# Splitting 18 more branch slabs of a two-block layer, and making 38 low parts with an accumulating transfer

## The chip, the cores and the metric

The program runs on one core of one Trainium2 chip. The metric is the device time of one execution in microseconds, the median of several runs. The numbers of the profile come from one profiled execution.

## The reference

The reference is two blocks of a language model over 256 tokens of width 2048, all in float32. The first block is a normalised input projection (2048 to 8192), a short gated convolution, attention with eight heads, and an output projection. The second block, where the change lies, computes:

```
h        = rmsnorm(x)
proj     = h @ w_in_2                     # 2048 -> 2048 (conv) + 1024 (ssm) + 4096 (gates)
b_conv   = silu(layernorm(conv31(glu(proj[:2048])))) @ conv_w_out
b_ssm    = (z @ w_val) * sigmoid(z @ w_gate),  z = gelu(state-space scan of proj[2048:3072])
gates    = sigmoid(proj[3072:] + b_gate)
x        = x + (gates0 * b_conv + gates1 * b_ssm) @ w_out
x        = x + peer(rmsnorm(x))           # picks 128 rows of a table for each token, twice
out      = rmsnorm(x)
```

## The kernel before

**Slabs.** Every weight matrix is cut into slabs of 128 partitions x 2048 float32 (1 MB). SP loads them one after the other (`load`, L356) into four buffers of `weight_raw`; the load of slab n waits until TensorE has finished the slab n-4. `weight_low` is declared over the same bytes as `weight_raw`. One slab gives one tile of 128 output channels x 256 tokens, summed over 16 blocks of the contraction.

**Two ways to multiply.** A plain tile (`tile`, L468) is 16 float32 matmuls of raw weight and operand. A split tile makes the same product out of float32r parts: the weight is high + low, the operand is high + low, and the tile is high*high + high*low + low*high. `split_product` issues 32 matmuls with the high part (L488, L489), and then, behind a wait on the low part, 16 matmuls with it (L492). `wide_product` (L508, L511) does the same with a double-width operand in other stages.

**Who makes the parts.** ACT makes the high part with a rounding copy from `weight_raw` into one of two buffers of `weight_high` (`split_high`, L761), once TensorE has finished the split tile two before. DVE subtracts it from the raw slab in place and so gives the low part (`split_low`, L1108).

**The branch and gate stages.** The first 24 slabs of `w_in_2` are the branch tiles, in the order of the list `BRANCH`: four conv tiles, ssm 0 to 3, twelve conv tiles, ssm 4 to 7. Twenty are plain; four (t = 6 to 9, from `SPLIT_AT`) are split. The 32 gate slabs behind them are all split. ACT goes through the tiles in order: `read_out` (L796) copies the finished tile out of PSUM, then `split_high` makes the high part of a slab that comes two later. After the branch tiles 5 to 8, TensorE multiplies the ssm inputs (L632) and ACT copies them out of PSUM (`ssm_inputs`, L761 on `work`). In the gate stage TensorE has extra work after gate 1 (`ssm_outputs`), gates 5 to 8 (`ssm_inputs`), gate 19 and gate 23 (layer-norm sums, L675 and L681).

**DVE beside them.** DVE's order is written out by hand: operand lows (L1389), convolution of two channels with their `split_low` calls, the first scan (L1406 to L1411, from `scan(0)`), three more convolutions (L1441) with the lows of gates 0 to 18 between the taps, then `scan(1)` with the lows of gates 19 to 31. Each `split_low` waits for ACT's high part of its slab. TensorE waits for DVE at gate 19 (`conv_done`), at `ssm_outputs(0)` after gate 1 and at `ssm_outputs(1)` after the 14th tile of the following stage.

**GpSimd.** POOL makes constants at the start and is then idle until the table rows are gathered (`gather`, L428: an indirect transfer of 128 rows of 8 KB, 1 MB, each).

Of the kernel before, what the change touches and what calls it, by code (L numbers as in the profile page):

```python
# [13 lines left out]
P = 128  # L14
# [48 lines left out]
def uses_before(b, s):  # L63
# [25 lines left out]
PLAIN = 2  # L89
SPLIT_OUT = 64 - PLAIN  # L90
SPLIT_BRANCH = SPLIT_OUT + 16
SPLIT_GATE = SPLIT_BRANCH + 4
SPLIT_VG = SPLIT_GATE + 32
SPLIT_OUT2 = SPLIT_VG + 16
SPLIT_AT = 6
SPLIT_SLABS = [*range(PLAIN, 80), *range(80 + SPLIT_AT, 80 + SPLIT_AT + 4), *range(80 + 24, 80 + 56), *range(80 + 56 + 8, 80 + 56 + 8 + 32)]
SPLIT_TILES = [*range(TILE_IN + PLAIN, TILE_IN2), *range(TILE_IN2 + SPLIT_AT, TILE_IN2 + SPLIT_AT + 4), *range(TILE_GATE, TILE_CV),
               *range(TILE_VG + 1, TILE_OUT2, 2), *range(TILE_OUT2, TILE_WQ)]

O_OUT, O_GATE, O_Z, O_OUT2 = KD, 2 * KD, 3 * KD, 3 * KD + KH  # L100


def split_in(t):

    return t - PLAIN


def split_tile(i):
# [4 lines left out]
def split_slab(i):  # L113

    return SPLIT_SLABS[i]

# [66 lines left out]
def build(nc, d):  # L183
    ctx = ExitStack()
    with ctx:
# [3 lines left out]
        def sem(name):  # L189
            return ctx.enter_context(nc.semaphore(name))  # L190
# [99 lines left out]
        eps_ready = sem("eps_ready")  # L290
        x_paired, x_squared = sem("x_paired"), sem("x_squared")
        proj_done, proj_freed = sem("proj_done"), sem("proj_freed")
        w_high_ready, w_low_ready = sem("w_high_ready"), sem("w_low_ready")
        o_high_ready, o_low_ready = sem("o_high_ready"), sem("o_low_ready")
        misc_done, misc_freed = sem("misc_done"), sem("misc_freed")
        bu_done, bu_freed, cy_done, skip_ready = sem("bu_done"), sem("bu_freed"), sem("cy_done"), sem("skip_ready")
# [108 lines left out]
        @block.gpsimd  # L405
        def _(pool):
            nc.gpsimd.memset(ident[:, :], 0.0).then_inc(consts_set, 1)
            nc.gpsimd.memset(ones[:, :], 1.0).then_inc(consts_ready, 1)
            pool.wait_ge(consts_set, 1)
            nc.gpsimd.affine_select(out=ident[:, :], in_=ident[:, :], compare_op=ALU.not_equal, fill=1.0, base=0,  # L410
                                    pattern=[[-1, P]], channel_multiplier=1).then_inc(consts_ready, 1)
            nc.gpsimd.memset(mask, 0.0).then_inc(mask_set, 1)
            pool.wait_ge(mask_set, 1)
            for lo in (0, 2 * P):
                nc.gpsimd.affine_select(out=mask[:, lo:lo + P], in_=mask[:, lo:lo + P], compare_op=ALU.is_ge,
                                        fill=-3.0e38, base=0, pattern=[[-1, P]],
                                        channel_multiplier=1).then_inc(mask_ready, 1)

            pool.wait_ge(merged, KD)
            nc.gpsimd.iota(iota16, pattern=[[1, 16]], base=0, channel_multiplier=0,  # L420
                           allow_small_or_imprecise_dtypes=True).then_inc(zero_ready, 1)
            nc.gpsimd.memset(zero_row, 0.0).then_inc(zero_ready, 1)
            def gather(s, col, table):

                b = ROW[s]
                if USES[s] > 0:
                    pool.wait_ge(row_free[b], USES[s])
                nc.gpsimd.indirect_dma_start(  # L428
                    rows[b], None, table, bass.IndirectOffsetOnAxis(ap=picks[:, col:col + 1], axis=0),
                ).then_inc(gathered[b], 16)  # L430

            for t in range(TT):
                for v, table in ((0, d["peer_u_2"][0]), (1, d["peer_v_2"][0])):
                    parts = [(*heads, n + 1) for n, heads in enumerate(HEAD_PARTS)] if t == v == 0 \
                        else [(0, PEER_H, len(HEAD_PARTS) + t)]
                    for first, last, ready in parts:
                        pool.wait_ge(picks_ready, ready)
                        for i in range(first * PEER_K, last * PEER_K):
                            s = (2 * t + v) * PICKS + i
                            if UNPACED <= s < EARLY_PICKS:  # L440
                                slab = SLAB_WQ + slab_before(s)
                                pool.wait_ge(raw_landed[slab % NSLAB], 16 * (slab // NSLAB + 1))
                            if s == EARLY_PICKS:
                                pool.wait_ge(proj_done, TILES)
                            gather(s, t * PICKS + i, table)
# [5 lines left out]
        def _(pe):  # L451
# [20 lines left out]
            def split_product(i, sub=0, kts=KD, order=None, ready=None, place=lambda k: k):  # L472

                per = SLAB // kts // P
                t = split_tile(i) - (per - 1) + sub
                if sub == 0:
                    slabs.append(t)
                at = split_slab(i) % NSLAB
                high, low = (w.rearrange("p (k n) -> p k n", k=kts)[:, :, sub * P:(sub + 1) * P]
                             for w in (w_high[:, i % NHIGH, :], w_low[:, at, :]))  # L480
                out = ps_p[:, (t - TILE_IN) % PSLOTS, :]
                order = list(range(kts)) if order is None else order
                pe.wait_ge(w_high_ready, i + 1)
                pe.wait_ge(proj_freed, t + 1)
                for k in order:
                    if ready is not None:
                        pe.wait_ge(o_low_ready, ready(k))
                    nc.tensor.matmul(out, high[:, k, :], o_high[:, place(k), :], start=(k == order[0]), stop=False)  # L488
                    nc.tensor.matmul(out, high[:, k, :], o_low[:, place(k), :], start=False, stop=False)  # L489
                pe.wait_ge(w_low_ready, i + 1)  # L490
                for k in order:
                    mm = nc.tensor.matmul(out, low[:, k, :], o_high[:, place(k), :], start=False, stop=(k == order[-1]))  # L492
                mm.then_inc(proj_done, 1)

            def wide_product(i, order=None, ready=None, place=lambda k: k):
# [9 lines left out]
                for k in order:  # L505
                    if ready is not None:
                        pe.wait_ge(o_low_ready, ready(k))
                    nc.tensor.matmul(out, high[:, k, :], o_parts[:, :, place(k), :], start=(k == order[0]), stop=False)  # L508
                pe.wait_ge(w_low_ready, i + 1)
                for k in order:  # L510
                    mm = nc.tensor.matmul(out[:, 1, :], low[:, k, :], o_high[:, place(k), :], start=False, stop=(k == order[-1]))  # L511
                mm.then_inc(proj_done, 1)
# [138 lines left out]
            pe.wait_ge(misc_freed, M_B + 4)  # L651
            first = BRANCH.index(("ssm", 0)) + 1
            for t in range(len(BRANCH)):
                if SPLIT_AT <= t < SPLIT_AT + 4:
                    split_product(SPLIT_BRANCH + t - SPLIT_AT, ready=(lambda k: O_GATE + k + 1) if t == SPLIT_AT else None)
                else:
                    tile(TILE_IN2, t, normed_in, ready=(lambda k: (h_scaled, KD + k + 1)) if t == 0 else None)
                if first <= t < first + 4:
                    ssm_inputs(t - first)

# [98 lines left out]
        def _(act):  # L759
# [8 lines left out]
            def split_high(i):  # L768

                s = split_slab(i)  # L770
                act.wait_ge(raw_landed[s % NSLAB], 16 * (s // NSLAB + 1))
                if i >= NHIGH:
                    act.wait_ge(proj_done, split_tile(i - NHIGH) + 1)
                act_copy(w_high[:, i % NHIGH, :], w_raw[:, s % NSLAB, :]).then_inc(w_high_ready, 1)

            def square(n, q0, src):

# [170 lines left out]

            first = BRANCH.index(("ssm", 0)) + 1
            for t, (kind, n) in enumerate(BRANCH):  # L950
                read_out(TILE_IN2, t, slot(BRANCH_SLOT[kind] + n), ACT.Sigmoid if kind == "sig" else ACT.Copy)
                if t in (SPLIT_AT - 3, SPLIT_AT - 2):
                    split_high(SPLIT_BRANCH + t - SPLIT_AT + 3)
                elif t in (SPLIT_AT, SPLIT_AT + 1):
                    split_high(SPLIT_BRANCH + t - SPLIT_AT + 2)
                if first <= t < first + 4:
                    ssm_inputs(t - first)
                elif first + 4 <= t < first + 8:
                    if t == first + 4:
                        act.wait_ge(rstd_ready, 12)  # L960
                    skip_matrix(t - first - 4)
                if t >= len(BRANCH) - 2:
                    split_high(SPLIT_GATE + t - (len(BRANCH) - 2))

            for t in range(32):
                dst = slot(GA0 + t) if t < KD else slot(gb(t - KD))
                read_out(TILE_GATE, t, dst, ACT.Sigmoid, bias=params[:, C_GATE + t:C_GATE + t + 1])
                if t < 30:
                    split_high(SPLIT_GATE + t + 2)
                if SSM_IN <= t < SSM_IN + 4:  # L970
                    ssm_inputs(t - SSM_IN + 4)
                elif t == SSM_OUT + 1:
# [99 lines left out]
        def _(dve):  # L1072
# [30 lines left out]

            def split_low(i):

                s = split_slab(i)
                dve.wait_ge(w_high_ready, i + 1)
                v.tensor_tensor(w_low[:, s % NSLAB, :], w_raw[:, s % NSLAB, :], w_high[:, i % NHIGH, :], ALU.subtract).then_inc(w_low_ready, 1)  # L1108
# [383 lines left out]
            for k in range(KD):  # L1492
                operand_low(O_GATE + k + 1, normed_in[:, k, :], k)
            conv(0, 1, 0, ())
            split_low(SPLIT_BRANCH)
            conv(1, 1, 0, ())
            for n in range(1, 4):
                split_low(SPLIT_BRANCH + n)
            scan(0)
            conv(2, 2, 0, LOW_LAGS[0])  # L1500
            conv(4, 2, 5, LOW_LAGS[1])
# [239 lines left out]
```

## Time and profile before

| what | value |
|---|---|
| median of 3 runs | 2513.13 us (2512.08 to 2514.20) |
| profiled execution | 2512.88 us, span 2511.1 us |
| PE busy | 1733.7 us (69%) |
| DVE busy | 1872.3 us (75%) |
| ACT busy | 564.1 us (22%) |
| POOL busy | 869.5 us (35%) |
| DMA | 747.83 MB, 51.5% of the engines' time for POOL's transfers, 22.9% for SP's |

The page averages over very different stages: projections up to about 1050 us, the routing and the gathers after that. The change touches the stretch from 515 to 888 us of the span (branch tiles, then gate tiles), so the rows are read there.

### The profile page before, as it was taken

What the parts mean: (1) busy time and instruction counts of PE and PEld (TensorE: products, weight loads), DVE (VectorE), ACT (ScalarE), POOL (GpSimd) and SP (SyncE); (2) the same over time, 40 slices, a digit from 0 to 9 for tenths busy, and PEclk for the clock granted to TensorE, in tenths of its full rate; (3) what the DMA queues carried; (4) which work ended last, traced back from release to release, by engine and by line L of the source; (5) the groups of instructions that cost most, each with busy time, mean ns of one, the idle gap of its engine ahead of it and who ended that gap; (6) DMA issues with size and microseconds to landing.
All of it is one profiled execution on the core that took longest, in us unless ns stands there. A gap on an engine that the chain in (4) does not pass through costs nothing. (4 is left out here: it accounts for less than half of the span.)

```text
span 2511.1 us, 22450 instructions
## 1 busy us (share of the span) xinstructions
PE 1733.7 (69%) x8754; PEld 1310.6 (52%) x8754; DVE 1872.3 (75%) x2486; ACT 564.1 (22%) x832; POOL 869.5 (35%) x524
## 2 busy tenths in 40 slices
PE   9999999999999999999920004777750000277776
PEld 8888887889889989888810001222220000022222
DVE  7757687688989885565999997777469999844444
ACT  4345555432143524432000001000000000100000
POOL 0000000000000000001458886655558888755552
PEclk9999999999999999999965557999985555599999
DMA  6544444534445444555989999999999999999997
GB/s 231 185 168 168 168 168 151 201 136 153 161 141 183 160 159 154 192 192 211 411 327 422 422 422 422 422 421 421 422 421 423 422 422 422 422 422 421 422 422 302
DMA packets 103495, 747.83 MB, mean 298 GB/s; under 512 B 11616, under 2 KB 11616, under 8 KB 12896
## 3 DMA queue, kind: packets, MB, share of 16 engines
q0 software_dynamic: 73728, 536.90, 51.5%
q1 hardware_dynamic: 29376, 209.20, 22.9%
q8 instruction: 69, 1.13, 0.2%
q10 hardware_dynamic: 288, 0.31, 0.0%
q14 instruction: 34, 0.28, 0.0%
HBM read 744.28 MB, written 2.10 MB: 297 GB/s over the span
## 5 line engine op out<-in xcount | busy, mean ns | idle before, releaser
L1108 DVE TENSOR_TENSOR weight_low<-weight_raw,weight_high 128x2048 fp32r<-128x2048 f32 x146 | 334.0, 2288 | 119.7 <-ACT weight_high L761 119.6
L747 PE MATMUL ps<-weight_raw,residual_t 128*128 128x512 f32 x368 | 171.3, 609 | 323.0 <-ACT residual_t L1058 265.0
L508 PE MATMUL ps<-operand_parts,weight_high 128*128 128x512 f32 x1504 | 370.9, 399 | 8.0 <-DVE operand_parts L1360 3.9
L420 POOL IOTA slots<- 128x16 f32 x1 | 0.1, 144 | 1043.3 <-DVE slots L1486 1043.3
L747 PE MATMUL ps<-rows_high,residual_t 128*128 128x512 f32 x192 | 92.2, 625 | 347.9 <-ACT residual_t L1058 317.4
L508 PEld LDWEIGHTS ps<-operand_parts,weight_high 128*128 128x128 f32 x1504 | 279.4, 189 | 70.5 <-issue 5.5
L761 ACT ACTIVATE weight_high<-weight_raw 128x2048 fp32r<-128x2048 f32 x146 | 278.6, 1908 | 97.1 <-PE ps L511 94.5
L747 PEld LDWEIGHTS ps<-weight_raw,residual_t 128*128 128x128 f32 x368 | 67.2, 192 | 427.2 <-ACT residual_t L1058 332.9
L747 PEld LDWEIGHTS ps<-rows_high,residual_t 128*128 128x128 f32 x192 | 36.1, 198 | 403.8 <-ACT residual_t L1058 347.7
L468 PE MATMUL ps<-slots,weight_raw 128*128 128x256 f32 x960 | 208.3, 379 | 0.9 <-DVE slots L1119 0.9
L488 PE MATMUL ps<-operand_parts,weight_high 128*128 128x256 f32 x832 | 204.2, 285 | 0.0
L489 PE MATMUL ps<-operand_parts,weight_high 128*128 128x256 f32 x832 | 202.5, 283 | 0.0
L1593 DVE SCALAR_TENSOR_TENSOR weight_raw<-weight_raw,work 128x2048 f32<-128x2048 f32 x85 | 193.4, 2290 | 11.7 <-DMA weight_raw<-in_peer_u,slots 11.7
L511 PEld LDWEIGHTS ps<-operand_parts,weight_low 128*128 128x128 f32 x1504 | 192.8, 191 | 7.5 <-DVE weight_low L1108 0.3
L468 PEld LDWEIGHTS ps<-slots,weight_raw 128*128 128x128 f32 x960 | 182.0, 190 | 26.2 <-issue 1.6
L511 PE MATMUL ps<-operand_parts,weight_low 128*128 128x256 f32 x1504 | 195.2, 283 | 0.0
L428 POOL DMA_INDIRECT weight_raw<-in_peer_u,slots x85 | 172.8, 2033 | 29.4 <-issue 25.3
L1593 DVE SCALAR_TENSOR_TENSOR slots<-slots,work 128x2048 f32<-128x2048 f32 x75 | 170.6, 2290 | 9.5 <-DMA slots<-in_peer_u,slots 9.4
L1611 DVE SCALAR_TENSOR_TENSOR work<-weight_raw,slots,work 128x2048 f32<-128x2048 f32 x45 | 105.8, 2352 | 93.9 <-DMA weight_raw<-in_peer_v,slots 93.6
L428 POOL DMA_INDIRECT slots<-in_peer_u,slots x75 | 147.9, 1973 | 59.5 <-issue 20.4
L428 POOL DMA_INDIRECT weight_raw<-in_peer_v,slots x91 | 129.7, 1425 | 99.5 <-PE ps L747 74.0
L488 PEld LDWEIGHTS ps<-operand_parts,weight_high 128*128 128x128 f32 x832 | 159.5, 192 | 3.2 <-issue 3.1
(230 smaller groups left out, 2950.4 us busy)
## 6 DMA issues: line engine op xcount, KB each, us to landing
weight_raw<-in_w_in SPq DMA_DIRECT2D x120, 1024.0 KB, 4.8
weight_raw<-in_w_out SPq DMA_DIRECT2D x32, 1024.0 KB, 4.8
weight_raw<-in_peer_w_q SPq DMA_DIRECT2D x16, 1024.0 KB, 8.5
weight_raw<-in_conv_w_out SPq DMA_DIRECT2D x8, 1024.0 KB, 4.8
weight_raw<-in_ssm_w_val SPq DMA_DIRECT2D x8, 1024.0 KB, 4.8
weight_raw<-in_ssm_w_gate SPq DMA_DIRECT2D x8, 1024.0 KB, 4.8
residual_t<-in_x SPq DMA_DIRECT2D x4, 512.0 KB, 5.9
out_y<-work SPq DMA_DIRECT2D x4, 512.0 KB, 5.2
```

The costliest lines, as they stand in the source:

```text
L420: nc.gpsimd.iota(iota16, pattern=[[1, 16]], base=0, channel_multiplier=0, allow_small_or_imprecise_dtypes=True).then_inc(zero_ready, 1)
L428: nc.gpsimd.indirect_dma_start(rows[b], None, table, bass.IndirectOffsetOnAxis(ap=picks[:, col:col + 1], axis=0),).then_inc(gathered[b], 16)
L468: mm = nc.tensor.matmul(ps_p[:, t % PSLOTS, :], w[:, k, :], operand[:, k, :], start=(k == order[0]), stop=(k == order[-1]))
L488: nc.tensor.matmul(out, high[:, k, :], o_high[:, place(k), :], start=(k == order[0]), stop=False)
L489: nc.tensor.matmul(out, high[:, k, :], o_low[:, place(k), :], start=False, stop=False)
L508: nc.tensor.matmul(out, high[:, k, :], o_parts[:, :, place(k), :], start=(k == order[0]), stop=False)
L511: mm = nc.tensor.matmul(out[:, 1, :], low[:, k, :], o_high[:, place(k), :], start=False, stop=(k == order[-1]))
L747: mm = nc.tensor.matmul(ps_v[:, c, :], diag[:, i // 2 % 16, :], rows[b][:, c * 512:(c + 1) * 512], start=False, stop=False, skip_group_che ...
L761: return nc.scalar.activation(dst, src, ACT.Copy)
L1108: v.tensor_tensor(w_low[:, s % NSLAB, :], w_raw[:, s % NSLAB, :], w_high[:, i % NHIGH, :], ALU.subtract).then_inc(w_low_ready, 1)
L1593: v.scalar_tensor_tensor(out=rows[b], in0=rows[b], scalar=1.0, in1=h_tok[:, t, :], op0=ALU.mult, op1=ALU.mult, accum_out=dots[:, at:at + 1 ...
L1611: v.scalar_tensor_tensor(out=y_tok[:, t, :], in0=rows[b], scalar=pick_w[:, at:at + 1], in1=y_tok[:, t, :], op0=ALU.mult, op1=ALU.add).then ...
```

## The change

The branch tiles 2 to 23 are split now (before: 6 to 9), so 22 instead of 4. For these 22 and for the gates 0, 2, ... 30 DVE's subtraction is left out. ACT writes the negated high part into the `weight_high` buffer; POOL then issues a transfer that loads the same slab from memory once more and adds it to what is in that buffer, which leaves the low part there. ACT makes the high part a second time, in place in the raw slab's buffer, after it has read the finished tile out. TensorE swaps the two buffers for these slabs and waits for the transfer's semaphore in place of DVE's.

```diff
-SPLIT_GATE = SPLIT_BRANCH + 4
+SPLIT_GATE = SPLIT_BRANCH + 22
+PLAIN2 = 2
+SPLIT_SLABS = [*range(PLAIN, 80), *range(80 + PLAIN2, 80 + 56), *range(80 + 56 + 8, 80 + 56 + 8 + 32)]
+LOW_BY_DMA = [*range(SPLIT_BRANCH, SPLIT_GATE), *range(SPLIT_GATE, SPLIT_VG, 2)]
...
+def lows_by_vector(i):
+    return i + 1 - sum(j <= i for j in LOW_BY_DMA)
...
+            for n, i in enumerate(LOW_BY_DMA):
+                t = split_tile(i) - TILE_IN2
+                kind, m = BRANCH[t] if t < len(BRANCH) else ("gate", t - len(BRANCH))
+                pool.wait_ge(minus_high, n + 1)
+                nc.gpsimd.dma_start(w_high[:, i % NHIGH, :], d["w_in_2"][BRANCH_SLAB.get(kind, 3 * KH) + m],
+                                    accum_op=ALU.add).then_inc(low_landed[i % NHIGH], 16)
...
+                parts = (w_low[:, at, :], w_high[:, i % NHIGH, :]) if by_dma else (w_high[:, i % NHIGH, :], w_low[:, at, :])
-                pe.wait_ge(w_low_ready, i + 1)
+                if by_dma:
+                    pe.wait_ge(low_landed[i % NHIGH], 16 * sum(j <= i and (i - j) % NHIGH == 0 for j in LOW_BY_DMA))
+                else:
+                    pe.wait_ge(w_low_ready, lows_by_vector(i))
...
+            def split_minus_high(i):
+                s = split_slab(i)
+                act.wait_ge(raw_landed[s % NSLAB], 16 * (s // NSLAB + 1))
+                act.wait_ge(proj_done, split_tile(i - NHIGH) + 1)
+                nc.scalar.activation(w_high[:, i % NHIGH, :], w_raw[:, s % NSLAB, :], ACT.Copy, scale=-1.0).then_inc(minus_high, 1)
+            def split_in_place(i):
+                s = split_slab(i)
+                act_copy(w_low[:, s % NSLAB, :], w_raw[:, s % NSLAB, :]).then_inc(w_high_ready, 1)
+            def read_and_split(i, tile0, n, dst, func=ACT.Copy, **kw):
+                if i in LOW_BY_DMA:
+                    split_minus_high(i)
+                    read_out(tile0, n, dst, func, **kw)
+                    split_in_place(i)
+                else:
+                    read_out(tile0, n, dst, func, **kw)
+                    if i < SPLIT_VG:
+                        split_high(i)
...
             def split_low(i):
+                if i in LOW_BY_DMA:
+                    return
...
             conv(0, 1, 0, ())
-            split_low(SPLIT_BRANCH)
             conv(1, 1, 0, ())
-            for n in range(1, 4):
-                split_low(SPLIT_BRANCH + n)
             scan(0)
```

The loops over the branch and gate tiles on ACT call `read_and_split` with the slab two tiles ahead.

## Rows read from the trace of the kernel before

**Rows 1.** The page: clock and DMA in 40 slices, queues
```profile
PEclk9999999999999999999965557999985555599999
DMA  6544444534445444555989999999999999999997
...
q0 software_dynamic: 73728, 536.90, 51.5%
q1 hardware_dynamic: 29376, 209.20, 22.9%
```
**Rows 2.** Windows: us, PE, PEld, DVE, ACT, POOL busy (count), clock, DMA share, GB/s
```profile
515.00:681.00 166.00, 166.00 (x897) 147.39 (x896) 147.43 (x307) 34.31 (x65) 0.00 (x0) 1.00 0.41 146
681.00:888.00 207.00, 205.44 (x1710) 197.03 (x1709) 182.92 (x306) 94.73 (x108) 0.00 (x0) 1.00 0.46 163
```
**Rows 3.** Timeline of ACT, branch stage: start, duration, what, idle before
```profile
572.62 2.05 ACT L761 ACTIVATE work<-ps 128x512 f32<-128x512 f32 x4
...
591.50 0.38 ACT L796 ACTIVATE slots<-ps 128x256 f32<-128x256 f32 x1 [6.24 <-PE ps L468]
...
598.40 0.38 ACT L796 ACTIVATE slots<-ps 128x256 f32<-128x256 f32 x1 [6.23 <-PE ps L468]
...
563.52 0.38 ACT L796 ACTIVATE slots<-ps 128x256 f32<-128x256 f32 x1 [3.85 <-PE ps L492]
...
570.54 0.38 ACT L796 ACTIVATE slots<-ps 128x256 f32<-128x256 f32 x1 [2.88 <-PE ps L492]
```
**Rows 4.** Timeline of ACT, gate stage
```profile
775.13 0.47 ACT L796 ACTIVATE slots<-ps,scan_ws 128x256 f32<-128x256 f32 x1 [3.48 <-PE ps L492]
775.50 1.91 ACT L761 ACTIVATE weight_high<-weight_raw 128x2048 fp32r<-128x2048 f32 x1
780.89 0.47 ACT L796 ACTIVATE slots<-ps,scan_ws 128x256 f32<-128x256 f32 x1 [3.48 <-PE ps L492]
```
**Rows 5.** Waits between 680 and 900 us: total, times, longest
```profile
DVE weight_low L1108 <- ACT weight_high L761: 22.9, 11, 7.2
...
PEld ps L492 <- DVE weight_low L1108: 1.8, 1, 1.8
```
**Rows 6.** Timelines of DVE (ends of convolutions and second scan) and of ACT
```profile
797.00 0.14 DVE L1503 COPY small<-small 128x1 f32<-128x1 f32 x1
...
813.14 0.38 ACT L977 ACTIVATE scan_ws<-ps 128x256 f32<-128x256 f32 x1 [1.18 <-PE ps L675]
...
932.09 0.15 DVE L1426 COPY small<-small 128x1 f32<-128x1 f32 x1
...
935.87 0.38 ACT L796 ACTIVATE operand<-ps 128x256 f32<-128x256 f32 x1 [3.07 <-PE ps L468]
```
**Rows 7.** Groups of DVE, 515 to 952 us
```profile
L1108 DVE TENSOR_TENSOR weight_low<-weight_raw,weight_high 128x2048 fp32r<-128x2048 f32 x38 | 86.8, 2286 | 27.6 <-ACT weight_high L761 27.5
```
**Rows 8.** Timeline of PE: one gate tile, its high part and its low part
```profile
700.67 0.39 PE L488 MATMUL ps<-operand_parts,weight_high 128*128 128x256 f32 x1
...
704.61 2.08 PE L492 MATMUL ps<-operand_parts,weight_low 128*128 128x256 f32 x16
706.52 0.28 PE L488 MATMUL ps<-operand_parts,weight_high 128*128 128x256 f32 x1
```
**Rows 9.** Source line 428, POOL's gathers of 1 MB: time from issue to landing
```profile
DMA to landing us min/median/max: 5.7/23.8/26.8
```
**Rows 10.** Timeline of POOL, first gathers
```profile
1172.82 0.94 POOL L428 DMA_INDIRECT rows_high<-in_peer_u,slots  x1 [0.30 <-issue]
```
**Rows 11.** DMA between 1300 and 1400 us: queue, packets, MB, share of 16 engines
```profile
q0 software_dynamic: 5750, 41.87, 101.1%
```
**Rows 12.** DMA between 515 and 681 us: queue, then SP's issues with us to landing
```profile
q1 hardware_dynamic: 3312, 24.12, 40.6%
...
weight_raw<-in_w_in SPq DMA_DIRECT2D x23, 1024.0 KB, 4.8
```
**Rows 13.** Timeline of ACT around gate 27
```profile
864.85 1.91 ACT L761 ACTIVATE weight_high<-weight_raw 128x2048 fp32r<-128x2048 f32 x1
866.78 1.28 ACT L987 ACT_TABLE_LOAD   x1
868.07 3.31 ACT L987 ACTIVATE slots<-slots,scan_ws 128x256 f32<-128x256 f32 x8
871.40 1.28 ACT L796 ACT_TABLE_LOAD   x1
```

More of the change, by code:

```diff
@@ L91 @@
 SPLIT_BRANCH = SPLIT_OUT + 16
-SPLIT_GATE = SPLIT_BRANCH + 4
+SPLIT_GATE = SPLIT_BRANCH + 22
 SPLIT_VG = SPLIT_GATE + 32
 SPLIT_OUT2 = SPLIT_VG + 16
-SPLIT_AT = 6
-SPLIT_SLABS = [*range(PLAIN, 80), *range(80 + SPLIT_AT, 80 + SPLIT_AT + 4), *range(80 + 24, 80 + 56), *range(80 + 56 + 8, 80 + 56 + 8 + 32)]
-SPLIT_TILES = [*range(TILE_IN + PLAIN, TILE_IN2), *range(TILE_IN2 + SPLIT_AT, TILE_IN2 + SPLIT_AT + 4), *range(TILE_GATE, TILE_CV),
+PLAIN2 = 2
+SPLIT_SLABS = [*range(PLAIN, 80), *range(80 + PLAIN2, 80 + 56), *range(80 + 56 + 8, 80 + 56 + 8 + 32)]
+SPLIT_TILES = [*range(TILE_IN + PLAIN, TILE_IN2), *range(TILE_IN2 + PLAIN2, TILE_CV),
                *range(TILE_VG + 1, TILE_OUT2, 2), *range(TILE_OUT2, TILE_WQ)]
+LOW_BY_DMA = [*range(SPLIT_BRANCH, SPLIT_GATE), *range(SPLIT_GATE, SPLIT_VG, 2)]
 O_OUT, O_GATE, O_Z, O_OUT2 = KD, 2 * KD, 3 * KD, 3 * KD + KH
@@ L292, in build @@
         proj_done, proj_freed = sem("proj_done"), sem("proj_freed")
-        w_high_ready, w_low_ready = sem("w_high_ready"), sem("w_low_ready")
+        w_high_ready, w_low_ready, minus_high = sem("w_high_ready"), sem("w_low_ready"), sem("minus_high")
+        low_landed = [sem(f"low_landed{n}") for n in range(NHIGH)]
         o_high_ready, o_low_ready = sem("o_high_ready"), sem("o_low_ready")
@@ L478, in split_product @@
                 at = split_slab(i) % NSLAB
-                high, low = (w.rearrange("p (k n) -> p k n", k=kts)[:, :, sub * P:(sub + 1) * P]
-                             for w in (w_high[:, i % NHIGH, :], w_low[:, at, :]))
+                by_dma = i in LOW_BY_DMA
+                parts = (w_low[:, at, :], w_high[:, i % NHIGH, :]) if by_dma else (w_high[:, i % NHIGH, :], w_low[:, at, :])
+                high, low = (w.rearrange("p (k n) -> p k n", k=kts)[:, :, sub * P:(sub + 1) * P] for w in parts)
                 out = ps_p[:, (t - TILE_IN) % PSLOTS, :]
@@ L508, in wide_product @@
                     nc.tensor.matmul(out, high[:, k, :], o_parts[:, :, place(k), :], start=(k == order[0]), stop=False)
[L509 removed]
+                pe.wait_ge(w_low_ready, lows_by_vector(i))
                 for k in order:
@@ L653, in _ @@
             for t in range(len(BRANCH)):
-                if SPLIT_AT <= t < SPLIT_AT + 4:
-                    split_product(SPLIT_BRANCH + t - SPLIT_AT, ready=(lambda k: O_GATE + k + 1) if t == SPLIT_AT else None)
+                if t < PLAIN2:
+                    tile(TILE_IN2, t, normed_in, ready=(lambda k: (h_scaled, KD + k + 1)) if t == 0 else None)
                 else:
-                    tile(TILE_IN2, t, normed_in, ready=(lambda k: (h_scaled, KD + k + 1)) if t == 0 else None)
+                    split_product(SPLIT_BRANCH + t - PLAIN2, ready=(lambda k: O_GATE + k + 1) if t == PLAIN2 else None)
                 if first <= t < first + 4:
@@ L950, in _ @@
             for t, (kind, n) in enumerate(BRANCH):
[L951 to L955, printed above, removed]
+                read_and_split(SPLIT_BRANCH + t, TILE_IN2, t, slot(BRANCH_SLOT[kind] + n), ACT.Sigmoid if kind == "sig" else ACT.Copy)
                 if first <= t < first + 4:
@@ L961, in _ @@
                     skip_matrix(t - first - 4)
-                if t >= len(BRANCH) - 2:
-                    split_high(SPLIT_GATE + t - (len(BRANCH) - 2))
             for t in range(32):
                 dst = slot(GA0 + t) if t < KD else slot(gb(t - KD))
-                read_out(TILE_GATE, t, dst, ACT.Sigmoid, bias=params[:, C_GATE + t:C_GATE + t + 1])
-                if t < 30:
-                    split_high(SPLIT_GATE + t + 2)
+                read_and_split(SPLIT_GATE + t + 2, TILE_GATE, t, dst, ACT.Sigmoid, bias=params[:, C_GATE + t:C_GATE + t + 1])
                 if SSM_IN <= t < SSM_IN + 4:
```

## The prediction

> **What bounds the kernel now.** I read the page first. From about 1250 us on the DMA line stands at eight or nine tenths [rows 1]: that half is gathers, the change does not touch it, and it starts only when the projections are done. So what the projections lose or gain should reach the end one for one. Then the windows of the two stages touched [rows 2]. In the branch stage (515 to 681 us) PE is busy 166.00 of 166 us, in the gate stage 205.44 of 207, both at a granted clock of 1.00, which is the 2.4 GHz level. DVE has 147.43 and 182.92 us of work, ACT far less, POOL none, and the DMA engines are busy 0.41 and 0.46 of the time. So TensorE's stream of matmuls is the bound, and everything else is cover. The waits confirm it: in the gate stage PE waited once for a low part, 1.8 us, while DVE waited 22.9 us for ACT's high parts [rows 5]. DVE follows PE there, it does not hold it back. Its two late deadlines hold too: the convolutions end at 797.0 us, and PE's sum over them, which asks for them, ends just before ACT reads it at 813.1; the second scan ends at 932.1 us, and the tile ahead of its use is read out at 935.9 [rows 6].
>
> **What the split itself gives.** A plain branch tile takes 598.40 - 591.50 = 6.90 us from one read-out to the next. A gate tile, which is split, takes 780.89 - 775.13 = 5.76 us [rows 3, 4]. A split branch tile with ssm inputs takes 570.54 - 563.52 = 7.02, so 1.26 us are the inputs [rows 3]. Eighteen more split tiles save 18 x (6.90 - 5.76) = 20.5 us, if PE waits for nothing new. The stage is then 2 x 6.90 + 22 x 5.76 + 4 x 1.26 = 145.6 us, against 20 x 6.90 + 4 x 5.76 + 4 x 1.26 = 166.1 before, which agrees with the window.
>
> **DVE** drops 20 subtractions: 36 before in these stages (4 branch, 32 gates; the 38 of the group include two of a later stage), 16 after. At 2.29 us each that is 46 us less work [rows 7]. This pays nothing on its own, as PE did not wait for DVE, but for the 1.8 us. It is what lets DVE's two deadlines come 20 us earlier: the odd gates' lows still wait for PE, the rest does not.
>
> **ACT.** Each of the 38 slabs takes a second copy of 1.9 us, 72 us in all. ACT's cycle per tile becomes 1.9 + 0.4 + 1.9 = 4.2 us in 5.76 [rows 4], or 6.3 of 7.02 beside the ssm inputs with their 2.05 us of copies [rows 3]. The high part is ready 4.2 us after the tile two before has ended, and PE asks at 5.76. So it is hidden, with 1.5 us to spare. The read-out is 1.9 us later and PE needs its PSUM bank only a whole tile later. The cover is gone in one place: at gate 27 ACT spends 5.9 us on table loads and eight Silu [rows 13]; I put 1 us there.
>
> **SP** issues as before. Its buffers are freed by the same tiles. **POOL** is idle, so the 38 issues queue behind nothing.
>
> **The new wait.** This carries the whole forecast. PE now waits, between the high part and the low part of a tile, for a chain: tile i-2 ends, ACT negates (1.9), POOL issues, the transfer lands (L), PE does 16 low matmuls. The high part of a tile takes 704.61 - 700.67 = 3.94 us and the low part 1.91 [rows 8]. So the low part is asked for 5.76 + 3.84 = 9.6 us after tile i-2 has ended, and L may be 9.6 - 1.9 - 0.1 = 7.6 us. Everything behind the waiting low matmuls on PE's queue waits too. The trace of before shows no accumulating transfer. The nearest row is a gather of the same 1 MB: 5.7 us from issue to landing at best, 0.94 of it POOL's own time [rows 9, 10]. With L = 5.7 the transfer is in time by 1.9 us. But an adding transfer also reads what it adds to: 1 MB from memory, 1 MB from SBUF, 1 MB written. In the saturated stretch 41.87 MB took 101.1% of 100 us, 2.53 us of all 16 engines per slab [rows 11]; a second read at that price makes L = 8.2, late by 0.6 us. The raw load of each slab overlaps in part and takes its turns on the same engines: half of its 2.9 us (40.6% of 166 us for 23 slabs [rows 12]) would be 1.4 more. The chain holds two tiles together: (1.9 + 0.1 + L + 1.9)/2 is 6.05 us per tile at L = 8.2 and 6.75 at 9.6.
>
> The second limit is the engines' own load. In the branch stage each tile brings a raw load and an adding one: 2.9 + 2 x 2.53 = 8.0 us of all engines if reads and writes add up wholly, 2.9 + 2.53 = 5.4 if the second read costs nothing. Both ends stay for the range. I take 7.0 us per tile, between the chain's 6.75 and the load's 8.0 and nearer to the chain, since part of the 2.9 us in a half-idle stage is waiting that a full queue would fill. In the gates two raw loads and one adding load take 2.9 x 2 + 5.1 = 10.9 of 11.5 us, so there the chain decides. I take L = 8.7 there: a pair of tiles takes 12.6 instead of 11.5 us, 1.1 lost. Of 16 pairs six have extra matmuls of 1.26 us or more in their window (the chain behind gates 0, 4, 6, 8, 18 and 22), which hide it. Ten remain.
>
> The Trainium skill, page "Collectives: The Full Stack", Part 3, section on the bandwidth ceiling, speaks against this change: the add inside the DMA engine costs nothing by itself, but its two source reads halve the rate. No run so far of this kernel shows it. By that rule the second read is paid in full (L = 8.2 and more); by the gather row alone it is not, and the sum is that of rival A.
>
> **Sum.** Branch: 2 x 6.90 + 22 x 7.0 + 4 x 1.26 = 172.8 against 166.1, +6.7 us. Gates: 10 x 1.1 = +11.0, less the 1.8 us that PE no longer waits, plus 1 at gate 27. Together +16.9 us on the profiled execution's 2512.9 us (span 2511.1), which lies 0.2 us under the median. That gives 2530 us.
>
> **Rivals.** A: the transfer is in time. The second read is hidden under the first, L stays at or under 7.6, and the stage runs at 5.76 us. For it: 5.7 us in rows 9, and DMA engines that are idle more than half of the time. Against it: the doubled reading. Then -20.5 - 1.8 = -22.3, 2490.6 us. This decides the sign: with nothing lost in the gates, the turn is at 6.78 us per branch tile ((166.1 - 18.8 + 1.8)/22).
>
> B: the adding transfer is far slower than two copies (row by row, read then write, little overlapped). From L = 12 on, a tile takes 8.0 us in the branch stage: +28.6 us, and each of the 16 gate pairs loses 4.4 us, 70 us less some 15 hidden: about 2595 us. Nothing in the trace excludes it; nothing shows it.
>
> C: PE's new gaps cost clock. In the second half of the page the clock falls to 5 where PE has nothing to do, from 9 where it works [rows 1]. Gaps of 1 to 2 us in each 7 are much shorter than those; but if the 1.2 GHz level came for a tenth of the two stages, each of those 37 us would do half its work, +19 us on top: 2549. The gate stage kept 1.00 with 1.6 us idle [rows 2].
>
> D: the edit has no effect on the sum: the branch stage turns from PE-bound to DMA-bound at about 6.8 us and the gates just keep up. Within 5 us of 2513.
>
> E: the transfer does not do what it says (each issue split in several, or POOL slow to build it, 3 us and more instead of 0.94). It would read as B in a weaker form, 2540 to 2570 us.
>
> **How the numbers follow.** 0.2% is 5 us, about what a measurement of this kernel can tell from no change. Chances: my case with its spread above +5 us 0.30; its lower edge where the branch stage gains a few us, faster than -5, 0.07; D 0.13; A 0.31; B 0.09; C 0.03; E 0.07. Faster 0.38, same 0.13, slower 0.49. The likeliest single case is mine, 2530. Its own range is 2505 (6.4 us per branch tile, gates level) to 2560 (8.0 us per tile: 194.8 us, +28.7, and gates +18). The whole range takes in A, 2488, and goes up through C and E to 2575; B's far end is left out.
>
> **What would show it.** In the profile after, PE's wait before the low matmuls L492 should be put down to a DMA into `weight_high`, 0.5 to 1.5 us per branch tile and about 1 us for every second gate. ACT's read-outs should be about 7.0 us apart in the branch stage, in the gates 11.5 to 12.6 for a pair. The branch window should show a DMA share above 0.85 against 0.41, and POOL's issues a landing of 8 to 10 us. DVE should have 20 subtractions fewer and finish its second scan earlier. If the landing is under 7.6 us, my second read is wrong and A has come. If the branch tiles lie 8 us and more apart with DMA engines not full, it is B. A clock under 0.95 in 515 to 900 us is C. A stall before L488, on the high part, would mean that I mispriced ACT.

## The result, and the profile after

The changed kernel takes 2550.77 us (median of 4 runs, 2543.03 to 2560.02) against 2513.66 before: ratio 1.0148, 95% interval 1.0135 to 1.0161. The profiled execution took 2551.71 us, its span is 2549.9 us. The change makes the kernel 37 us slower; its four runs scatter over 17 us, so the time is known to some 3 us (the interval). The forecast was 2530 us: the right sign, and less than half of the size.

The page after, clock and DMA in 40 slices, queues, and the group of the new transfers (answers to [rows 1]):

```profile
PEclk9999999999999999999985555999995555599999
DMA  5544444589978754554989999999999999999997
...
q0 software_dynamic: 79200, 576.75, 58.7%
q1 hardware_dynamic: 29376, 209.20, 22.3%
...
weight_high<-in_w_in POOLq DMA_DIRECT2D x38, 1024.0 KB, 10.3
```

The new part is the hump of 8, 9, 9, 7, 8, 7 in the DMA line, where 4 and 5 stood. POOL's queue moved 39.85 MB more, 38 slabs. The transfers of the two stages land a median of 10.3 us after POOL's issue.

The windows of the two stages after, in the columns of [rows 2]:

```profile
516.20:701.00 184.80, 155.97 (x1183) 148.11 (x1183) 139.38 (x309) 107.79 (x106) 19.93 (x23) 0.96 0.97 258
701.00:920.00 219.00, 204.16 (x1655) 193.76 (x1654) 143.51 (x257) 120.88 (x121) 12.78 (x15) 0.98 0.78 224
```

PE is no longer the bound of the branch stage: 156 us of work in 184.8 us, with the DMA engines busy 0.97 of the time. The granted clock is below 1.00 in both stages, which it was not before.

ACT's timeline after, the tiles around the end of the branch stage, the last gate, and POOL's first gather (answers to [rows 3, 4]; the last row is POOL's timeline):

```profile
694.14 1.92 ACT L799 ACTIVATE weight_high<-weight_raw 128x2048 fp32r<-128x2048 f32 x1 [3.74 <-PE ps L510]
695.97 0.36 ACT L837 ACTIVATE slots<-ps 128x256 f32<-128x256 f32 x1
696.23 1.90 ACT L779 ACTIVATE weight_low<-weight_raw 128x2048 fp32r<-128x2048 f32 x1
701.41 0.38 ACT L837 ACTIVATE slots<-ps 128x256 f32<-128x256 f32 x1 [3.28 <-PE ps L510]
...
926.58 0.47 ACT L837 ACTIVATE slots<-ps,scan_ws 128x256 f32<-128x256 f32 x1 [5.29 <-PE ps L510]
```
```profile
1210.20 1.05 POOL L442 DMA_INDIRECT rows_high<-in_peer_u,slots  x1 [124.75 <-DVE slots L1607]
```

The same three points in the trace of the kernel before:

```profile
681.28 0.39 ACT L796 ACTIVATE slots<-ps 128x256 f32<-128x256 f32 x1 [4.72 <-PE ps L468]
...
887.52 0.47 ACT L796 ACTIVATE slots<-ps,scan_ws 128x256 f32<-128x256 f32 x1 [5.29 <-PE ps L492]
```
```profile
1171.42 1.09 POOL L428 DMA_INDIRECT rows_high<-in_peer_u,slots  x1 [125.02 <-DVE slots L1575]
```

The first three ACT rows after the change are its cycle: negate, read out, copy in place. The last branch tile is read out at 701.41 us; before it was 681.28. Of the 20.1 us between, 1.2 had already come before the stage (the table load ahead of the first block's last square starts at 505.69 instead of 504.51; why is not shown), so the branch stage costs 18.9. The last gate is read out at 926.58 against 887.52, so the gates cost another 18.9. The first gather starts 38.8 us later than before (1210.20 against 1171.42), and the spans differ by 38.8. So next to nothing is won or lost behind the gates.

The waits after, first 516 to 701 us, then 701 to 922 us (answers to [rows 5]):

```profile
PEld ps L510 <- DMA weight_high<-in_w_in: 33.1, 21, 3.5
DVE scan_ws L1441 <- ACT work L779: 28.5, 1, 28.5
...
PE ps L510 <- DMA weight_high<-in_w_in: 28.4, 17, 3.3
```
```profile
PEld ps L510 <- DMA weight_high<-in_w_in: 17.0, 11, 2.9
PE ps L510 <- DMA weight_high<-in_w_in: 14.8, 10, 2.7
```

L510 is the line of the low matmuls, so this is the new wait where the prediction put it. PE waits 28.4 us in the branch stage for 22 slabs and 14.8 us in the gates. DVE gained the time that it was meant to gain and spends it waiting: 28.5 us ahead of its first scan alone (5.7 before), since PE delivers the ssm inputs too late. So its second scan ends at 969.1 us and not, as forecast, earlier than the 932.1 of before.

### The profile page after: what moved, and what is told of

The parts are those of the page before. It is cut to its first block and busy times, and to the rows that moved or that the text cites. A ratio compares the mean times of both kernels' runs of the same rounds, so it can differ in the third digit from the quotient of the medians.

```text
span 2549.9 us, 23117 instructions
## 1 busy us (share of the span) xinstructions
PE 1738.4 (68%) x9042; PEld 1319.2 (52%) x9042; DVE 1829.0 (72%) x2466; ACT 666.4 (26%) x888; POOL 910.7 (36%) x562
## 5 line engine op out<-in xcount | busy, mean ns | idle before, releaser
L1143 DVE TENSOR_TENSOR weight_low<-weight_raw,weight_high 128x2048 fp32r<-128x2048 f32 x126 | 288.5, 2290 | 176.3 <-ACT weight_high L779 176.3
L430 POOL DMA_DIRECT2D weight_high<-in_w_in x38 | 32.7, 861 | 876.1 <-ACT weight_high L799 876.1
L526 PEld LDWEIGHTS ps<-operand_parts,weight_high 128*128 128x128 f32 x1504 | 278.6, 189 | 69.9 <-issue 5.0
L779 ACT ACTIVATE weight_high<-weight_raw 128x2048 fp32r<-128x2048 f32 x126 | 240.4, 1908 | 94.5 <-PE ps L529 94.5
L529 PE MATMUL ps<-operand_parts,weight_low 128*128 128x256 f32 x1504 | 195.2, 283 | 0.0
L1091 ACT ACTIVATE residual_t<-ident,slots 128x128 f32<-128x128 f32 x128 | 48.1, 398 | 432.9 <-PE ps L765 432.1
L765 PE MATMUL ps<-slots,residual_t 128*128 128x512 f32 x272 | 126.3, 607 | 40.3 <-DMA slots<-in_peer_v,slots 40.3
L503 PE MATMUL ps<-operand_parts,weight_low 128*128 128x256 f32 x608 | 150.7, 288 | 0.0
L504 PE MATMUL ps<-operand_parts,weight_low 128*128 128x256 f32 x608 | 149.0, 285 | 0.0
L442 POOL DMA_INDIRECT rows_high<-in_peer_u,slots x48 | 92.3, 1924 | 152.0 <-DVE slots L1607 124.7
## 6 DMA issues: line engine op xcount, KB each, us to landing
weight_high<-in_w_in POOLq DMA_DIRECT2D x38, 1024.0 KB, 10.3
```

The costliest lines, as they stand in the source:

```text
L430: nc.gpsimd.dma_start(w_high[:, i % NHIGH, :], d["w_in_2"][BRANCH_SLAB.get(kind, 3 * KH) + m], accum_op=ALU.add).then_inc(low_landed[i % N ...
L442: nc.gpsimd.indirect_dma_start(rows[b], None, table, bass.IndirectOffsetOnAxis(ap=picks[:, col:col + 1], axis=0),).then_inc(gathered[b], 16)
L765: mm = nc.tensor.matmul(ps_v[:, c, :], diag[:, i // 2 % 16, :], rows[b][:, c * 512:(c + 1) * 512], start=False, stop=False, skip_group_che ...
L779: return nc.scalar.activation(dst, src, ACT.Copy)
L1091: nc.scalar.activation(diag[:, i // 2 % 16, :], ident[:, :], ACT.Copy, scale=pick_w[:, t * P + i:t * P + i + 1]).then_inc(diag_ready, 1)
```

## The experiments

Theory 1 throughout is that of the prediction, made sharper by the trace after: an adding transfer costs twice the DMA time of a copy; 22 of them in a row fill the DMA engines, and in the gates each arrives too late for a buffer that turns over in two tiles.

**e1: the transfers in the branch stage only.**

```diff
-LOW_BY_DMA = [*range(SPLIT_BRANCH, SPLIT_GATE), *range(SPLIT_GATE, SPLIT_VG, 2)]
+LOW_BY_DMA = [*range(SPLIT_BRANCH, SPLIT_GATE)]
```

> The 22 branch slabs keep the adding transfer; all 32 gates go back to DVE's subtraction. Theory 1 (each stage pays on its own, by the transfer in it): the branch stage still takes about 185 us against 166 before, the gate stage goes back to about 206 us, and the time is 2513.7 + 19 = about 2533 us. Theory 2 (the gates were slow because of something the branch stage leaves behind, such as DVE's later order): the gate stage stays above 215 us and the time stays above 2543 us.

Measured: 2534.59 us, ratio 1.0093 (1.0071 to 1.0116). The windows of e1, the two stages:

```profile
516.00:701.00 185.00, 156.15 (x1182) 149.03 (x1181) 140.43 (x307) 105.03 (x102) 19.03 (x22) 0.95 0.97 256
701.00:909.00 208.00, 206.44 (x1713) 197.90 (x1713) 181.34 (x305) 94.76 (x108) 0.00 (x0) 1.00 0.46 163
```

The branch stage is as bad as in the full change. The gate stage is back at that of before, 208 against 207 us, with PE busy and at full clock. Theory 1 holds.

**e2: the transfers in the gates only.** The branch stage's list, loops and subtractions are those of before.

```diff
-LOW_BY_DMA = [*range(SPLIT_BRANCH, SPLIT_GATE), *range(SPLIT_GATE, SPLIT_VG, 2)]
+LOW_BY_DMA = [*range(SPLIT_GATE, SPLIT_VG, 2)]
```

> The branch stage is that of before (four slabs split, DVE's subtraction); every second gate keeps the adding transfer. Theory 1: the branch stage takes 166 us, the gate stage about 225 us as in the changed kernel, the time is about 2533 us. Theory 2 (the gates are slow only behind a branch stage that fills the DMA engines): the gate stage takes 208 us or less, the time is 2515 us.

Measured: 2532.93 us, ratio 1.0076 (1.0059 to 1.0092). The windows of e2:

```profile
515.00:681.30 166.30, 165.79 (x896) 147.11 (x895) 147.69 (x311) 36.44 (x66) 1.11 (x1) 1.00 0.44 152
681.30:907.00 225.70, 210.67 (x1708) 200.42 (x1707) 151.64 (x300) 121.39 (x122) 12.78 (x15) 0.98 0.76 219
```

The gate stage is slow by itself, behind a branch stage that is not touched and with DMA engines busy 0.76. The two parts cost 21 and 19 us alone, 40 together, against the 37 measured for both. So they are two losses, each there without the other.

**e3: copy in place of add.** The low part of 38 slabs is then the slab itself, so everything behind it works on other values. From the first gather to the end its trace takes 1339.3 us against 1339.7 before, so the time can still be compared.

```diff
-                                    accum_op=ALU.add).then_inc(low_landed[i % NHIGH], 16)
+                                    ).then_inc(low_landed[i % NHIGH], 16)
```

> All 38 transfers copy the slab and do not add, so the low parts are wrong; everything else is as in the changed kernel. Theory 1 (the second read is the price): the landing falls from a median of 10.3 to under 7.6 us, the DMA share of the branch stage from 0.97 to 0.90 or less, no wait is left before the low matmuls, and the time is 2513.7 - 22 = about 2491 us. Theory 2 (what costs is POOL's path and its fixed latency, not the adding): the landing stays above 8.5 us and the time above 2530 us. In between: the share of the 57 us that goes is the share of the second read.

Measured: 2506.97 us, ratio 0.9972 (0.9961 to 0.9982). The groups of DMA issues of e3, and its queues between 530 and 655 us, followed by those of the changed kernel over the same stretch:

```profile
weight_high<-in_w_in POOLq DMA_DIRECT2D x38, 1024.0 KB, 5.8
...
q1 hardware_dynamic: 2995, 21.91, 49.0%
q0 software_dynamic: 2895, 20.97, 44.8%
```
```profile
q0 software_dynamic: 2288, 16.65, 66.2%
q1 hardware_dynamic: 2302, 16.77, 34.0%
...
weight_high<-in_w_in POOLq DMA_DIRECT2D x15, 1024.0 KB, 10.9
```

The time from issue to landing over all 38 transfers, in e3 and then in the changed kernel:

```profile
DMA to landing us min/median/max: 5.0/5.8/7.8
```
```profile
DMA to landing us min/median/max: 7.9/10.3/13.9
```

Copying, the transfers land after 5.8 us (5.0 to 7.8), adding after 10.3 (7.9 to 13.9). A copied slab holds all 16 engines for 0.448 x 125 / 20.0 = 2.80 us, an added one for 0.662 x 125 / 15.9 = 5.21 us. POOL's own instruction takes 0.53 us for a copy against 0.85. With copies no wait for a transfer is left, and the branch stage takes 146.7 us; the prediction's sum for the split alone was 145.6.

But the time is 2507 and not 2491. The windows of e3, branch stage and the stretch behind it, and its longest wait of PE:

```profile
516.00:662.70 146.70, 146.15 (x1186) 142.36 (x1187) 121.08 (x266) 108.14 (x106) 12.42 (x23) 1.00 0.90 327
662.70:687.60 24.90, 13.39 (x97) 13.19 (x96) 24.69 (x56) 6.28 (x6) 0.53 (x1) 0.80 0.39 143
```
```profile
PE ps L510 <- DVE weight_low L1143: 11.5, 1, 11.5
```

PE arrives at gate 1 while DVE is still in its first scan; the low part of gate 1 stands behind that scan and 14 taps of a convolution in DVE's order. That deadline was not in the prediction at all.

**e4: half of the columns added.**

```diff
-                nc.gpsimd.dma_start(w_high[:, i % NHIGH, :], d["w_in_2"][BRANCH_SLAB.get(kind, 3 * KH) + m],
+                nc.gpsimd.dma_start(w_high[:, i % NHIGH, 0:SLAB // 2], d["w_in_2"][BRANCH_SLAB.get(kind, 3 * KH) + m][:, 0:SLAB // 2],
```

> Each of the 38 transfers adds only the first 1024 of 2048 columns, so the low parts are wrong in the other half; POOL still issues one transfer per slab. Theory 1 (the price is bytes that are read and written, on top of a fixed part): the added load is half, 2.6 us of all engines, the sum with the raw slab 5.3 us per branch tile, under 5.76; the landing is about 6.5 to 7 us; no wait is left before the low matmuls, and the time is that of the copying kernel, about 2507 us, with the same wait of 11.5 us for DVE's low part of gate 1. Theory 2 (adding has a fixed cost per transfer, whatever its size): the landing stays above 8.5 us and the time above 2530 us.

Measured: 2507.58 us, ratio 0.9975 (0.9965 to 0.9985), landing 6.6 us (5.5 to 7.9). PE still waits 1.4 us in all for transfers, and 9.7 us for DVE's low part of gate 1 (11.5 expected). Queues of e4 between 530 and 655 us:

```profile
q0 software_dynamic: 2848, 10.36, 47.8%
q1 hardware_dynamic: 2931, 21.39, 46.6%
```

Half a slab added holds the engines 0.478 x 125 / 19.8 = 3.02 us, a whole one 5.21. So the second half costs 2.2 us, and by an estimate from these two sizes some 0.8 us of a transfer do not depend on its size. Most of the price goes by the bytes, as theory 1 has it, though my 2.6 us for the half was too low. POOL's instruction still takes 0.85 us here, so it is not what made the full transfers late.

**e5: filler matmuls ahead of each wait.**

```diff
                 if by_dma:
+                    for _ in range(10):
+                        nc.tensor.matmul(ps_m[:, 0, 0:T], high[:, 0, :], o_high[:, 0, :], start=True, stop=True)
                     pe.wait_ge(low_landed[i % NHIGH], ...
```

> The changed kernel with 10 more matmuls of 128x256 (1.2 us at full clock) ahead of each wait for a transfer, so that TensorE's gaps are shorter; they are written to an unused PSUM bank. Theory 1 (the branch stage is bound by the DMA engines, the clock's falls add a few us in the gates only): branch stage 183 to 187 us, granted clock 0.99 or more in both stages, gate stage 2 to 5 us shorter, time 2546 to 2550 us. Theory 2 (the falls of the clock behind gaps of 3 us make a third or more of the loss): branch stage 175 us or less, time 2538 us or less.

Measured: 2555.9 us, ratio 1.0167 (1.015 to 1.0184). The windows of e5:

```profile
516.20:703.00 186.80, 179.44 (x1440) 172.88 (x1439) 140.67 (x307) 108.70 (x104) 19.83 (x23) 1.00 0.98 262
703.00:928.00 225.00, 218.47 (x1791) 208.57 (x1791) 143.68 (x271) 119.20 (x120) 12.78 (x15) 0.99 0.75 213
```

The clock of the branch stage is back at 1.00, PE is busy 179 of 187 us, and the stage is not a microsecond shorter. So the fallen clock there was free. That the DMA engines bind the stage is read from their busy share, 0.98; the fillers alone would not tell their load from the chain of negation, transfer and low part. In the gates my number was wrong: ten fillers take 1.2 us, and only six of the 16 transfers there had kept PE waiting for longer than that, so they lengthened the path.

**e10: six fillers, transfers in the gates only** (e2 with `range(6)` as in e5).

> The kernel with the transfers in the gates only (2533 us), with 6 more matmuls of 128x256 (0.7 us at full clock) ahead of each wait for a transfer. Theory 1 (where a transfer lands late TensorE idles over 2 us, its clock falls to the lower level and costs some us): granted clock of the gate stage 1.00 against 0.98, time 2529 to 2531 us. Theory 2 (the clock costs nothing that counts, the chain of buffer, transfer and low part does): 2533 us or more.

Measured: 2530.04 us, ratio 1.0065 (1.0051 to 1.0079); the gate stage's clock is 1.00. That is 3 us under e2, in the direction of theory 1, but the two intervals overlap. The windows of e2 give the same size: in its gate stage the granted clock is below 1.00 in two stretches only, 799 to 803 and 871 to 875 us, which lose 3.4 us of full clock together. So the clock costs the gates about 3 us, and the rest of their loss is the waiting.

**e6: only the even branch tiles split, with the transfer started three tiles ahead.** `BRANCH_SPLIT = [*range(2, 24, 2)]`; the gates have DVE's subtraction.

```diff
+                read_out(TILE_IN2, t, ...)
+                if t + 3 in BRANCH_SPLIT:
+                    split_minus_high(SPLIT_BRANCH + BRANCH_SPLIT.index(t + 3))
+                    split_in_place(SPLIT_BRANCH + BRANCH_SPLIT.index(t + 3))
```

> Only the even branch tiles 2 to 22 are split (11, seven more than before the change), all with the adding transfer, which ACT starts three tiles ahead, so that a plain tile lies between two of them and the buffer turns over in four tiles; all gates have DVE's subtraction. Theory 1 (a transfer of 8 to 10 us is harmless where the engines have room and the buffer is free early): no wait for a transfer, plain and split tiles at 6.9 and 5.76 us, the branch stage 7 x 1.14 = 8 us shorter than before, up to 2 us given back at gate 1's low part: 2513.5 - 6 to - 8 = 2505 to 2507 us. Theory 2 (an adding transfer disturbs the raw loads or TensorE by its presence alone): waits remain, 2513 us or more.

Measured: 2512.01 us, ratio 0.9991 (0.9982 to 1.0000): a miss by 5 us. The waits for a transfer are indeed gone (0.6 us in all), though it lands after 8.8 us (8.2 to 11.4), and the branch stage ends 6.8 us earlier. The waits of e6 show where it goes:

```profile
ACT weight_high L800 <- DMA weight_raw<-in_w_in: 9.8, 7, 2.4
...
PE ps L511 <- DVE weight_low L1151: 4.5, 2, 3.0
```

PE waits 4.5 us for DVE's low parts at the first gates, the deadline that e3 had shown; that takes back most of the 6.8. ACT, three tiles ahead, waits 9.8 us for raw slabs that have not landed; whether that is why the branch stage gains 6.8 us and not 8 is not shown.

**e7: all 22 split, no transfer.** `LOW_BY_DMA = []`, with the 22 subtractions put between DVE's taps and scan steps.

> 22 branch slabs split as in the change, but no transfer adds: DVE makes all 54 low parts, those of the branch between the taps of its first two convolutions and the steps of its first scan. Theory 1 (without relief DVE becomes the bound): 18 more subtractions of 2.2 us delay DVE by about 30 us net at the first scan's end; TensorE waits for it at gate 1 and gate 19, gains 20 us in the branch stage and gives 20 to 40 us back, 2515 to 2535 us. Theory 2 (DVE has idle time enough to take them): 2500 us or less.

Measured: 2537.5 us, ratio 1.0096 (1.008 to 1.0111). The wait of PE in e7:

```profile
PE ps L510 <- DVE weight_low L1143: 32.5, 15, 5.2
```

DVE is the bound, and already in the branch stage, which ends at 696.6 us (681.3 before), not only at the gates as I had it. The time is 2.5 us above the upper end of my range.

**e9: e3 with DVE's low part of gate 1 moved ahead.**

```diff
-LOW_LAGS = ((10, 14, 21, 25, 29), ...
+LOW_LAGS = ((0, 1, 21, 25, 29), ...
```

> The copying kernel (transfers copy and do not add, low parts wrong) with DVE's low part of gate 1 moved from the 14th to the 1st tap behind its first scan. It measures what the change could give if every transfer were in time. Theory 1 (in the copying kernel the 11.5 us at gate 1 were DVE's order and nothing else): the wait shrinks to 3 us or less, and the time falls from 2507 to 2496 to 2499 us. Theory 2 (the scan itself ends too late): the wait stays above 6 us and the time above 2502 us.

Measured: 2495.74 us, ratio 0.9927 (0.9912 to 0.9943). PE's wait for DVE is 2.2 us. This is what the full split would be worth if every transfer landed as a copy does and DVE's order were mended: 17.5 us.

**e8: the mixed version.** Branch tiles 2 to 9 with DVE's subtraction, the odd tiles 11 to 23 with the transfer three tiles ahead.

```diff
+BRANCH_SPLIT = [*range(2, 10), *range(11, 24, 2)]
+LOW_BY_DMA = [*range(SPLIT_BRANCH + 8, SPLIT_GATE)]
+LOW_LAGS = ((0, 5, 18, 24, 29), ...
...
+            split_low(SPLIT_BRANCH)
+            conv(0, 1, SPLIT_BRANCH - SPLIT_GATE + 1, (7, 17, 27))
+            conv(1, 1, SPLIT_BRANCH - SPLIT_GATE + 4, (4, 13, 24))
+            split_low(SPLIT_BRANCH + 7)
             scan(0)
```

> Branch tiles 2 to 9 are split with DVE's subtraction (eight; DVE idles there before its first scan), the odd tiles 11 to 23 with the adding transfer started three tiles ahead (seven), the gates with DVE, their first two low parts 8 us earlier in DVE's order. 11 more split tiles than before the change. Theory 1 (as for the alternate kernel, and DVE's first scan starts some 4 us earlier): 11 x 1.14 + 1.8 = 14 us less, 2499 to 2502 us. Theory 2 (DVE's scans become the bound where the branch stage is over 8 us shorter): 2505 us or more, with a wait at gate 1 or 19.

Measured: 2502.34 us, ratio 0.9955 (0.9941 to 0.9969), 11.5 us faster than the kernel before, and the fastest here that leaves nothing out of the computation. The windows of e8:

```profile
515.60:675.00 159.40, 158.98 (x1115) 149.38 (x1116) 150.30 (x296) 69.45 (x85) 6.24 (x7) 1.00 0.68 205
675.00:877.00 202.00, 200.44 (x1667) 192.03 (x1667) 188.59 (x322) 92.58 (x106) 0.00 (x0) 1.00 0.46 162
```

PE is busy nearly all the time at full clock again (159.0 of 159.4 us in the branch stage), while the seven transfers land in a median of 9.4 us and PE waits for none of them.

**e11: e8 without its seven transfers** (`BRANCH_SPLIT = [*range(2, 10)]`).

> The mixed kernel without its seven slabs with an adding transfer: branch tiles 2 to 9 split with DVE's subtraction, the other 16 plain. Theory 1 (each split tile pays 1.14 us whoever makes its low part, if that is in time): 7 x 1.14 = 8 us slower than the mixed kernel's 2502.3, about 2510 us, of which 3 us may be hidden in the waits for DVE that the mixed kernel still has: 2507 to 2510 us. Theory 2 (the gain of the mixed kernel comes from DVE's earlier order alone): 2502 to 2504 us.

Measured: 2510.57 us, ratio 0.9988 (0.9979 to 0.9997). It is 8.2 us over e8, and seven split tiles at 1.14 us are 8.0. So of the 11.5 us that e8 gains, some 8 come from the seven tiles whose low parts the transfers make. Whether DVE could have made these seven in time as well was not run: e7 shows only that it cannot make 18 more.

## Why the prediction was right in sign and short in size

**PE-bound before, one for one to the end: right.** The gathers start 38.8 us later and the spans differ by as much.

**The split's worth: right.** 1.14 us per tile; e3's branch stage is 146.7 us against my 145.6, and e8 less e11 is 8.2 us for seven tiles.

**ACT, SP and POOL hidden: right.** No wait for the high part of a transferred slab is in the trace after, and POOL waits for ACT 38 times of 38.

**The adding transfer: right in kind.** Its best landing is 7.9 us in the changed kernel and 8.2 in e6, where I had worked out L = 8.2 from a gather and a second read. Part of that agreement is luck: the copy's best is 5.0 us and not the gather's 5.7, and the second read adds 2.9 us to it at best and not 2.53. The price of a second read, 2.53 us, came out as 5.21 - 2.80 = 2.4. The Trainium skill, "Collectives: The Full Stack", Part 3, the section on the bandwidth ceiling, has, for a ReduceScatter, the two source reads halving the rate; 5.21/2.80 = 1.86 agrees with it here.

**The step that failed is the size of the new wait, in both of its terms.** In the branch stage I took 7.0 us per tile, a value between the buffer's chain (6.75) and the load of the DMA engines (8.0), and leaned to the chain, since I held part of a raw slab's 2.9 us to be waiting. Measured is (701.41 - 530.05 - 4 x 1.26)/22 = 7.56 us, from the read-out of the second tile to that of the last:

```profile
530.05 0.38 ACT L837 ACTIVATE slots<-ps 128x256 f32<-128x256 f32 x1 [0.87 <-PE ps L482]
```

The load sets it: the queues between 530 and 655 us give 5.21 + 2.66 = 7.87 us of all engines per tile, at a busy share that sums to 1.00, for tiles that took 125/16 = 7.8 us there, ssm inputs included. The raw slab's 2.9 us shrank only to 2.66 in the full queue. The chain gives no other answer: with the landing of 10.9 us in that stretch it comes to (1.9 + 0.3 + 10.9 + 1.9)/2 = 7.5 us (POOL starts 0.3 us after the negation, not 0.1), and with the 8.2 us of e2, where the engines have room, to 6.15. So the landing is long because the engines are full. By the load of 7.87 us more buffers could not have brought the 22 tiles under that time, but this is an estimate; no run has a third buffer, or an early start with every tile split. The term is short by 22 x 0.56 = 12.3 us, of the 38.8 - 16.9 = 21.9 us by which the sum misses the profiled execution; 1.2 us came before the stage.

In the gates I had 11.0 us for ten pairs, less 1.8, plus 1, together 10.2, and measured is 18.9: 8.7 us short. Six of the ten pairs are right, 0.9 to 1.5 us lost in each (ACT's negations at 797.58, 810.01 and 822.58 us are 12.4 and 12.6 us apart, I had said 12.6). The other four lose 12 us together. Gate 0 loses 2.0 us; in e2, where no transfer of the branch stage runs ahead of it, it loses 0.1. At the gates 12, 18 and 28 the transfer lands 9.4 to 10.0 us after POOL's issue, and PE waits 2.1, 2.7 and 2.6 us; why it is late there is not shown. The pairs that end there take 14.4, 14.5 and 15.6 us, and behind two of these waits, at gates 12 and 28, the clock falls to 0.50 for some 3.5 us each time. Of the six pairs that I took for hidden, the one of gate 6 loses 1.7 us. The 1.8 us of before were won back at gate 27, and the next pair lost 4. The 1 us for the table loads does not show: PE waits for no high part there.

**Rival A was priced too well.** Even with every transfer in time the kernel stops at gate 1 for DVE's order, 11.5 us (e3), so the change as written could at best reach 2507, not 2490.6. I had checked DVE's deadlines at gate 19 and at the second scan's end [rows 6], but not those of the low parts that it still makes, which stand behind the first scan. A stage that is 20 us shorter brings every one of them forward.

**Rival B and E: no.** POOL's instruction takes 0.85 us. The landing has a median of 10.3 us (single ones reach 13.9), an added slab takes less of the DMA engines than two copies (5.21 against 5.60 us), and where the branch tiles lie 7.8 us apart the engines are full. **Rival C: real, and nearly free.** The clock is 0.96 and 0.98, but in the branch stage e5 shows that it costs nothing; in the gates of the changed kernel it is below 1.00 from 796 to 800 and from 905 to 909 us only, 3.4 us of full clock out of the 18.9. **Rival D** had the right mechanism for the branch stage, DMA-bound, at 7.56 and not 6.8.

## What to carry to other kernels

Price a transfer that adds as two reads: here it held the DMA engines 1.86 times as long as a copy and landed about 3 us later where the engines had room (8.8 us in e6 against 5.8 in e3), 4.5 us later in the full queue. Then add up the load of the engines per unit of work before asking about latency. Give it its buffer several tiles ahead, and use it only for as many tiles as the engines have room for; every second tile with an early start made PE wait for next to nothing here (0.6 us), where every tile cost 19 us. The spacing and the early start were changed together, so which of the two is needed is not shown. When a stage gets shorter, go through every deadline of the engine that works beside it, in its own order, and not only through the two that were late before.

## What was not expected of the hardware

The clock can fall behind quite short gaps, and after work has been taken up again. The timeline of PE in the changed kernel, gate 12:

```profile
792.27 0.28 PE L503 MATMUL ps<-operand_parts,weight_low 128*128 128x256 f32 x1
792.39 0.28 PE L504 MATMUL ps<-operand_parts,weight_low 128*128 128x256 f32 x1
...
794.74 2.74 PE L510 MATMUL ps<-operand_parts,weight_high 128*128 128x256 f32 x16 [2.07 <-DMA weight_high<-in_w_in]
797.28 0.41 PE L503 MATMUL ps<-operand_parts,weight_high 128*128 128x256 f32 x1
797.49 0.41 PE L504 MATMUL ps<-operand_parts,weight_high 128*128 128x256 f32 x1
```

PE is idle for 2.07 us, takes up work again at 794.74, and only then does the clock fall: the next matmuls start 0.21 us apart where they stood 0.12 apart before. That is the 1.2 GHz level. The granted clock of half-microsecond windows of the same stretch shows it:

```profile
795.50:796.00 0.50, 0.50 (x6) 0.50 (x6) 0.50 (x2) 0.00 (x0) 0.00 (x0) 1.00 0.04 16
796.00:796.50 0.50, 0.50 (x5) 0.50 (x4) 0.50 (x3) 0.00 (x0) 0.00 (x0) 0.56 0.04 16
796.50:797.00 0.50, 0.50 (x4) 0.50 (x4) 0.50 (x3) 0.00 (x0) 0.00 (x0) 0.50 0.00 0
```

So a stall of 2 us can be paid twice, once as the gap and once in the matmuls behind it, unless something else binds the stage anyway. The length of the gap does not tell which one: in the branch stage the clock fell behind a gap of 1.96 us and stayed at 1.00 behind one of 3.22, and at gate 18 it stayed at 1.00 behind one of 2.69. What decides is not shown here.
